# The first MLP product by one level of Strassen's rule, in 258-token tiles

## The chip, the cores and the metric

The kernel runs on one core of one Trainium2 chip. The metric is the device time of one execution in microseconds. The hardware profile is of one execution. TensorE is shown as two rows: PE for the matmuls, PEld for the loads of the stationary operand; DVE is VectorE, ACT is ScalarE, POOL is GpSimd, SP is SyncE, which issues most transfers.

## The reference

One decoder layer over 1024 prompt tokens and 8 decode tokens, 1032 in all, of width 1024, with shared weights. A wide projection feeds a pooling branch, a chunked mLSTM with four heads and an attention into 256 memory tokens; their outputs are gated, merged and projected. The change touches what comes last:

```python
x = x + rmsnorm(merged @ w_out, g_post_mix)
h2 = rmsnorm(x, g_pre_mlp)
f = jnp.square(jax.nn.relu(h2 @ w_ff1)) @ w_ff2      # w_ff1 (1024, 4096), w_ff2 (4096, 1024)
x = x + rmsnorm(f, g_post_mlp)
```

All is fp32. The kernel keeps that precision with a split: an operand is held as a rounded high part and a low part (the rest), and a product is three matmuls: high by high, low by high, high by low.

## The kernel before

Everything is feature-major: 128 features on the partitions, 1032 tokens along the row, in three groups of 344 (`tok[g]`). Weights come as slabs of 128 x 1024 values (`w_raw`, two slots), loaded by SP; GpSimd, at times ScalarE, makes the high part `w_hi` and GpSimd the low part `w_lo` (`split`, `split_merge`). All engines run lists written out by hand, one block per engine, with semaphores between them; loops (`Fori`) repeat three times in the MLP.

The work ends so. TensorE forms z = merged @ w_out in groups of 24 matmuls of 344 columns (8 blocks of the contraction, 3 passes). ScalarE copies and squares z, VectorE scales it by the inverse deviation (`z_scale`, recorded at line 1178, the helper of all scalar_tensor_tensor operations), GpSimd adds it to x (`x_in`, line 541): that is x1. ScalarE squares x1 into a ring, TensorE sums the squares over the features with a matrix of ones (line 838), ScalarE takes the root, VectorE the reciprocal (line 1525) and scales x1 into `acc`; ScalarE makes `h_hi`, VectorE and GpSimd four blocks of `h_lo` each (lines 1531 and 547). All of this goes group by group.

The MLP runs in eight chunks of 512 hidden features. `ff1` makes four column blocks for three groups: 24 matmuls each; ScalarE takes relu out of the bank, VectorE squares (1540), ScalarE rounds to `f_hi` and VectorE makes `f_lo` (1542), in two halves by turns. `ff2` takes the chunk of before in eight blocks by three groups of 12 matmuls, and VectorE adds each bank to `acc` (line 1552). On TensorE every matmul of a split product is recorded at line 581. In the tail the squares of the last blocks are summed by matmuls (`f_mean`, line 887), VectorE takes a reciprocal for each group (line 1570) and scales, and VectorE and GpSimd add x1 back.

GpSimd has two operations of 1024 elements for every slab. In SP's queue the slabs stand in order, each behind the split of the one before last.

## Time and profile before

| | |
|---|---|
| time, median of 3 runs | 2194.12 us (2193.63 to 2194.25) |
| profiled execution: span | 2186.1 us |
| what lies around the span, against the median | 8.0 us |
| TensorE matmuls busy | 2065.8 us (94%) |
| VectorE, GpSimd, ScalarE busy | 965.5, 801.9, 458.5 us |
| first matmul of the MLP | 1420.0 us |
| DMA | 180.16 MB, 82 GB/s over the span |

A matmul is recorded longer than the distance to the next one, since they are pipelined: the pace is read from starts, not from the mean length. A chain of waits is followed back from the end. Idle time of an engine that is not on that chain costs nothing.

### The profile page before, as it was taken

The page shows a single profiled execution, that of the slowest core. Times are in us where ns is not written, and L with a number is a line of the kernel's source. Part 1 is how long each engine was busy: PE and PEld are TensorE (multiplying, and loading weights), DVE is VectorE, ACT ScalarE, POOL GpSimd, SP SyncE. Part 2 cuts the span into 40 slices and gives each one's busy share as a digit, 9 for nine tenths or more (in the row PEclk, how much of TensorE's full clock was granted, in tenths as well). Part 3 has the DMA queues.
Part 4 walks back from the last instruction along what each step waited for, and adds up shares of the span by engine and source line. Part 5 has one row for each costly group of instructions (what it writes and reads, how often), then busy time and mean ns, then how long its engine had stood idle before and what let it go on. Part 6 is the DMA issues. An engine that isn't in the chain of part 4 may idle for free.

```text
span 2186.1 us, 32789 instructions
## 1 busy us (share of the span) xinstructions
PE 2065.8 (94%) x12821; PEld 2006.9 (92%) x12821; DVE 965.5 (44%) x1884; ACT 458.5 (21%) x880; POOL 801.9 (37%) x407
## 2 busy tenths in 40 slices
PE   5799999999999999999899989599999999999996
PEld 3799999999999999999889889399999999999995
DVE  6602552055403551155666741974334343443426
ACT  4411220122012220122046422431101010110101
POOL 4553323323333233332522233754334343343433
PEclk8899999999999999999889999799999999999998
DMA  3221331123211331123645331121111111111132
GB/s 136 68 81 60 111 125 64 39 102 115 97 39 64 125 125 40 49 102 125 223 133 162 97 128 47 58 78 43 45 49 50 48 39 50 49 49 44 44 116 78
DMA packets 64142, 180.16 MB, mean 82 GB/s; under 512 B 6648, under 2 KB 22264, under 8 KB 63400
## 3 DMA queue, kind: packets, MB, share of 16 engines
q1 hardware_dynamic: 57664, 154.46, 20.9%
q10 hardware_dynamic: 6376, 24.14, 2.8%
q8 instruction: 88, 1.44, 0.3%
q14 instruction: 14, 0.11, 0.0%
HBM read 141.83 MB, written 36.75 MB: 82 GB/s over the span
## 4 chain that ended last, share of the span: by engine, by line
PE 85%; DVE 9%; issue 2%; ACT 2%; DMA 1%; POOL 1%; SPq 0%; DVEq 0%; ACTq 0%; POOLq 0%
PE bank L581 77%; DVE acc L1178 2%; PE bank L705 1%; PE bank L708 1%; DVE x_in L1178 1%; PE bank L693 1%; PE bank L664 1%; PE bank L701 1%; PE bank L696 1%; DMA x_in<-xT 1%; PE bank L703 0%; PE bank L778 0%; PE bank L838 0%; PE bank L801 0%; PE bank L745 0%
## 5 line engine op out<-in xcount | busy, mean ns | idle before, releaser
L581 PE MATMUL bank<-h_hi,w_hi 128*128 128x344 f32 x2520 | 823.5, 327 | 29.1 <-DVE h_lo L1193 14.5
L581 PE MATMUL bank<-h_lo,w_hi 128*128 128x344 f32 x2520 | 807.6, 320 | 0.0
L581 PE MATMUL bank<-h_hi,w_lo 128*128 128x344 f32 x2520 | 805.8, 320 | 0.4 <-issue 0.4
L478 POOL TENSOR_TENSOR w_hi<-w_raw,ones 128x1024 fp32r<-128x1024 f32 x152 | 288.8, 1900 | 1193.1 <-PE bank L581 1180.4
L581 PEld LDWEIGHTS bank<-h_hi,w_hi 128*128 128x128 f32 x2520 | 475.8, 189 | 36.8 <-DVE h_lo L1193 15.0
L581 PEld LDWEIGHTS bank<-h_hi,w_lo 128*128 128x128 f32 x2520 | 475.4, 189 | 2.3 <-issue 1.0
L581 PEld LDWEIGHTS bank<-h_lo,w_hi 128*128 128x128 f32 x2520 | 475.7, 189 | 0.0
L480 POOL TENSOR_TENSOR w_lo<-w_raw,w_hi 128x1024 fp32r<-128x1024 f32 x152 | 371.6, 2445 | 11.9
L581 PE MATMUL bank<-f_hi,w_hi 128*128 128x344 f32 x768 | 246.4, 321 | 0.0
L581 PE MATMUL bank<-f_hi,w_lo 128*128 128x344 f32 x768 | 245.4, 320 | 0.0
L581 PE MATMUL bank<-f_lo,w_hi 128*128 128x344 f32 x768 | 245.2, 319 | 0.0
L1552 DVE TENSOR_TENSOR acc<-acc,bank 128x344 f32<-128x344 f32 x192 | 97.1, 511 | 230.0 <-PE bank L581 229.9
L1540 DVE TENSOR_TENSOR sqv<-rl 128x344 f32<-128x344 f32 x96 | 93.0, 969 | 142.2 <-ACT rl L904 141.8
L581 PEld LDWEIGHTS bank<-f_hi,w_hi 128*128 128x128 f32 x768 | 144.4, 188 | 0.8
L581 PEld LDWEIGHTS bank<-f_lo,w_hi 128*128 128x128 f32 x768 | 144.3, 188 | 0.0
L581 PEld LDWEIGHTS bank<-f_hi,w_lo 128*128 128x128 f32 x768 | 144.0, 188 | 0.2
L904 ACT ACTIVATE rl<-bank 128x344 f32<-128x344 f32 x96 | 43.8, 457 | 421.9 <-PE bank L581 421.9
L1542 DVE TENSOR_TENSOR f_lo<-sqv,f_hi 128x344 fp32r<-128x344 f32 x96 | 98.6, 1027 | 53.6 <-ACT f_hi L1139 53.6
L904 ACT ACTIVATE side_t<-bank 128x344 f32<-128x344 f32 x96 | 43.9, 458 | 309.1 <-PE bank L581 309.1
L1312 DVE TENSOR_TENSOR SW<-bank,SW 128x128 f32<-128x128 f32 x32 | 9.3, 292 | 143.1 <-ACT SW L1017 143.1
L1139 ACT ACTIVATE f_hi<-sqv 128x344 fp32r<-128x344 f32 x96 | 47.2, 492 | 117.7 <-DVE sqv L1540 117.7
L904 ACT ACTIVATE o_h<-bank 128x344 f32<-128x344 f32 x40 | 18.3, 459 | 234.3 <-PE bank L581 230.5
(293 smaller groups left out, 2442.2 us busy)
## 6 DMA issues: line engine op xcount, KB each, us to landing
w_raw<-w_stream SPq DMA_DIRECT2D x161, 512.0 KB, 3.3
d_side<-side_t ACTq DMA_DIRECT2D x32, 516.0 KB, 2.7
gates<-d_side SPq DMA_DIRECT2D x24, 344.0 KB, 4.2
dC<-stC SPq DMA_DIRECT2D x32, 256.0 KB, 3.4
qkb<-d_qk SPq DMA_DIRECT2D x32, 256.0 KB, 4.0
o_C_s<-dC SPq DMA_DIRECT2D x32, 256.0 KB, 2.0
x_in<-xT SPq DMA_DIRECT2D x3, 1376.0 KB, 11.2
gates<-d_side SPq DMA_DIRECT2D x8, 516.0 KB, 4.0
```

Source lines behind the costliest of these rows:

```text
L478: pool.tensor_tensor(w_hi[:, slot, :], w_raw[:, slot, :], ones[:, 0:1].to_broadcast([P, 1024]), ALU.mult).then_inc(s_hi_made, 1)
L480: pool.tensor_tensor(w_lo[:, slot, :], w_raw[:, slot, :], w_hi[:, slot, :].bitcast(F32), ALU.subtract)\
L581: last = pe.matmul(out, st, mv, start=i == 0, stop=i == n - 1)
L664: last = pe.transpose(b_tr[r][:, (c % 2) * 256 + k * P:(c % 2) * 256 + (k + 1) * P], src[:, k, c * L:(c + 1) * L], ident[:, :])
L693: last = pe.matmul(b_S[:, 0:L], ks[:, k, :], qs[:, k, :], start=k == 0, stop=k == 1)
L696: pe.matmul(b_W[:, 0:L], ones[0:4, :], A_pick[:, :], start=False, stop=True).then_inc(s_logw_ready, 1)
L904: act.activation(out, bank[g + 3 * second][:, 0:G], func, scale=scale).then_inc(s_group_free[g], 1)
L1139: act.activation(f_hi[:, half, j, tok[g]], sqv[:, g, :], ACT.Copy).then_inc(s_f_hi, 1)
L1178: return dve.scalar_tensor_tensor(out=out, in0=in0, scalar=scalar, in1=in1, op0=op0, op1=op1)
L1540: dve.tensor_tensor(sqv[:, g, :], rl[:, g, :], rl[:, g, :], ALU.mult).then_inc(s_relu_squared, 1)
L1542: dve.tensor_tensor(f_lo[:, half, j, tok[g]], sqv[:, g, :], f_hi[:, half, j, tok[g]].bitcast(F32), ALU.subtract).then_inc(s_f_lo, 1)
L1552: dve.tensor_tensor(acc[:, j, tok[g]], acc[:, j, tok[g]], bank[g + 3 * second][:, 0:G], ALU.add).then_inc(s_group_free[g], 1)
```

## The change

The first product is cut into halves in all three directions. Weights: two column blocks of w_ff1 form a pair, 16 in all, with two halves of the contraction; x1 has the same two contraction halves and two token halves of 516, each worked in two tiles of 258. One level of Strassen's rule gives each pair 7 products instead of 8. Each product needs a sum or difference of quarters of the weights (`W_OF`, 5 of 7; made on GpSimd per pair, in a ring of 8 slots of 512) and of x1 (`B_OF`, 5 of 7; made once on VectorE, in `build`, and kept). A product is 12 matmuls for each tile (4 contraction blocks, 3 passes), into a ring of 8 banks. ScalarE copies the first three products' tiles (`copy_c`), VectorE adds or subtracts the others (`combine`; steps d, e and f read a bank). At the end of a quarter, step u does relu and the scaling by the inverse deviation of x1; ScalarE squares it into a stage (`make_f`), and SP writes two rows of 1032 to DRAM for each pair (`store_f`).

So x1 is no longer scaled ahead of the product: ScalarE writes x1 times the gain into `acc`. The combining tiles `c_t` and the weights of odd pairs (`w_pairB`) also lie in acc's room, and the sums are made out of acc in the first pair. The second product runs after the first, in four chunks of 1024 hidden features: 32 units of three groups of 24 matmuls, whose rows are read back from DRAM and split again (ScalarE high, GpSimd low). The first chunk's rows land over the operands of the first product, as its last pair frees them. Loops in this part are written out. Semaphores are shared more widely elsewhere in the kernel, without a change of order there. `f_mean` is one matmul for each group, of squares that VectorE has summed, and the order of the last blocks changes.

The diff, cut to its core:

```diff
+        W_OF = [((0, 0), ALU.add, (1, 1)), ((1, 1), None, None), ((0, 0), ALU.add, (0, 1)), ((0, 1), ALU.subtract, (1, 1)),
+                ((0, 0), None, None), ((1, 0), ALU.add, (1, 1)), ((1, 0), ALU.subtract, (0, 0))]
+        B_OF = [((0, 0), ALU.add, (1, 1)), ((1, 0), ALU.subtract, (0, 0)), ((1, 1), None, None), ((1, 0), ALU.add, (1, 1)),
+                ((0, 1), ALU.subtract, (1, 1)), ((0, 0), None, None), ((0, 0), ALU.add, (0, 1))]
...
+        def w_quarter(i, q):
+            return (w_raw, w_pairB)[i % 2][:, q[0], 512 * q[1]:512 * q[1] + 512]
+
+        def b_quarter(q, s):
+            return acc[:, 4 * q[0]:4 * q[0] + 4, HALF * q[1] + Q4 * s:HALF * q[1] + Q4 * (s + 1)]
...
+        C_STEPS = [(1, 0, "d"), (1, 1, "d"), (2, 0, "d"), (2, 1, "d"), (3, 0, "d"), (3, 1, "d"), (3, 0, "u"), (3, 1, "u"),
+                   (4, 0, "f"), (4, 0, "e"), (4, 1, "f"), (4, 1, "e"), (4, 0, "u"), (4, 1, "u"),
+                   (5, 0, "f"), (5, 0, "e"), (5, 1, "f"), (5, 1, "e"), (5, 0, "u"), (5, 1, "u"),
+                   (6, 0, "e"), (6, 1, "e"), (6, 0, "u"), (6, 1, "u")]
...
+
+            i, p, s = t // 14, t % 14 // 2, t % 2
+            copied = 6 * i + 2 * p + s + 1 if p < 3 else 0
+            stepped = c_step(i, (p, s, "d" if p < 4 else "e")) if p else 0
+            return copied, stepped
...
+            def pair(i):
+                if i == 0:
+                    sp.wait_ge(s_slab_split, SLAB_FF)
+                elif i == 1:
+                    sp.wait_ge(s_b_lo, 10)
+                else:
+                    sp.wait_ge(s_wc_sum, 5 * (i - 1))
+                    sp.wait_ge(s_wc_lo, 7 * (i - 2) + 5)
+                sp.dma_start((w_raw, w_pairB)[i % 2][:, :, :],
+                             w_stream[SLAB_FF + 2 * i:SLAB_FF + 2 * i + 2].rearrange("a p c -> p a c"))\
+                    .then_inc(s_pair_loaded[i % 2], 16)
+
+            def store_f(i):
+                sp.wait_ge(s_f_made, 8 * (i + 1))
+                for m in range(2):
+                    sp.dma_start(d_f[2 * i + m], f_st[i % 2][m]).then_inc(s_f_stored[i % 2], 16)
...
+            for i in range(PAIRS - 1):
+                if i + 2 < PAIRS:
+                    pair(i + 2)
+                store_f(i)
+            for r in range(4):
+                sp.wait_ge(s_tile, 14 * (PAIRS - 1) + 2 * r + 2)
+                if r >= 2:
+                    sp.wait_ge(s_f_row_hi, 2 * r - 2)
+                sp.dma_start(f0_raw[:, 2 * r:2 * r + 2, :], d_f[2 * r:2 * r + 2].rearrange("a p t -> p a t"))\
+                    .then_inc(s_f_row[r % 2], 16)
+                if r >= 2:
+                    w2_slab(3 - r)
...
+                    sp.wait_ge(s_f_row_hi, 8 + u if j < 2 else 7 + u)
+                    sp.dma_start(f_raw[(c + 1) % 2][:, j, :], d_f[8 * (c + 1) + j]).then_inc(s_f_row[j % 2], 16)
...
+            def wc_sum(n):
+                i, p = n // 7, n % 7
...
+                pool.wait_ge(s_pair_loaded[i % 2], 16 * (i // 2 + 1))
+                if n == 5:
+                    pool.wait_ge(s_group_ready[2], UNIT_OUT + 8)
+                elif n >= RING:
+                    pool.wait_ge(s_tile, 2 * (n - RING) + 2)
+                pool.tensor_tensor(ring_sum[n % RING], w_quarter(i, a), w_quarter(i, b), op).then_inc(s_wc_sum, 1)
+
+            def wc_lo(n):
+                i, p = n // 7, n % 7
+                pool.wait_ge(s_wc_hi, n + 1)
+                t = w_quarter(i, W_OF[p][0]) if W_OF[p][1] is None else ring_sum[n % RING]
+                pool.tensor_tensor(ring_lo[n % RING], t, ring_hi[n % RING].bitcast(F32), ALU.subtract).then_inc(s_wc_lo, 1)
...
+            for n in range(4, 7 * PAIRS):
+                wc_sum(n + 1)
+                wc_lo(n)
...
+            for r in range(6):
+                f_row_lo(r, r + 1)
+                if r >= 4:
+                    w2_split(r - 4)
+            w2_split(2)
+            for u in range(32):
+                if u + 3 < 32:
+                    w2_split(u + 3)
+                if u < 24:
+                    f_row_lo(8 + u, 8 + u + 1)
...
-            def ff1(n, slots, t, first=0):
-                for j in range(first, 4):
-                    pe.wait_ge(s_slab_split, n + j + 1)
-                    for g in range(NG):
-                        h_group(slots[j], g, t + j)
...
+            for i in range(PAIRS):
+                for p in range(7):
+                    n = 7 * i + p
+                    pe.wait_ge(s_wc_lo, n + 1)
+                    for s in range(2):
+                        t = 2 * n + s
+                        if i == 0:
+                            pe.wait_ge(s_b_lo, 2 * p + s + 1)
+                        if t >= 8:
+                            copied, stepped = tile_read(t - 8)
+                            if copied:
+                                pe.wait_ge(s_c_copied, copied)
+                            if stepped:
+                                pe.wait_ge(s_c_step, stepped)
+                        product(bank[t % 8][:, 0:Q4],
+                                [(ring_hi[n % RING][:, k * P:(k + 1) * P], ring_lo[n % RING][:, k * P:(k + 1) * P],
+                                  b_hi[p][:, k, sub[s]], b_lo[p][:, k, sub[s]]) for k in range(4)]).then_inc(s_tile, 1)
+
+            def ff2_group(u, g, bank_of=None):
+                c, slot = u // 8, u % 4
+                group(g, UNIT_FF + u, [(w2_hi[slot][:, k * P:(k + 1) * P], w2_lo[slot][:, k * P:(k + 1) * P],
+                                        f_hi[c % 2][:, k, tok[g]], f_lo[c % 2][:, k, tok[g]]) for k in range(KD)], True, bank_of)
+            pe.wait_ge(s_c_step, c_step(PAIRS - 1, (4, 0, "e")))
+            pe.wait_ge(s_f_row_lo_dve, 2)
+            for u in range(28):
+                if u % 8 == 0:
+                    pe.wait_ge(s_f_row_lo, 6 + u)
+                pe.wait_ge(s_w2_lo, u + 1)
+                for g in range(NG):
+                    ff2_group(u, g)
...
+                if op is None:
+                    act.wait_ge(s_pair_loaded[i % 2], 16 * (i // 2 + 1))
+                    if n == 4:
+                        act.wait_ge(s_group_ready[2], UNIT_OUT + 8)
+                    elif n >= RING:
+                        act.wait_ge(s_tile, 2 * (n - RING) + 2)
+                    src = w_quarter(i, a)
+                else:
+                    act.wait_ge(s_wc_sum, wc_sums(n))
+                    src = ring_sum[n % RING]
+                act.activation(ring_hi[n % RING], src, ACT.Copy).then_inc(s_wc_hi, 1)
+
             for i, (j, g) in enumerate(z_last):
...
                     act.activation(sq_ring(i % 6), x_in[:, k, tok[g]], ACT.Square).then_inc(s_x1_sq, 1)
-                    if g == 1 and k == 3:
-                        x1_root(0)
+                    act.activation(acc[:, k, tok[g]], x_in[:, k, tok[g]], ACT.Copy, scale=vec[:, V_MLP + k:V_MLP + k + 1])\
+                       .then_inc(s_xg, 1)
+                    if g and k == 3:
...
+                    t = 14 * i + 2 * p + s
+                    if i:
+                        act.wait_ge(s_f_made, 8 * (i - 1) + 7 - 2 * p + s)
+                    act.wait_ge(s_tile, t + 1)
+                    act.activation((c1, c4, c5)[p][s], bank[t % 8][:, 0:Q4], ACT.Copy).then_inc(s_c_copied, 1)
...
+                if p == 3 and i >= 2:
+                    act.wait_ge(s_f_stored[i % 2], 32 * (i // 2))
+                for s in range(2):
+                    act.wait_ge(s_c_step, c_step(i, (p, s, "u")))
+                    act.activation(f_st[i % 2][m][:, HALF * half + Q4 * s:HALF * half + Q4 * (s + 1)], src[s], ACT.Square)\
+                       .then_inc(s_f_made, 1)
...
+            b_high(0)
+            for i in range(PAIRS):
+                for p in range(7):
+                    n = 7 * i + p
+                    if i == 0 and p == 0:
+                        b_high(1)
+                        wc_high(4)
+                        wc_high(5)
+                        for q in (2, 3, 4):
+                            b_high(q)
+                    elif i == 0 and p == 1:
+                        b_high(5)
+                    wc_high(n + 6)
+                    if i == 0 and p == 0:
+                        act.wait_ge(s_b_lo, 10)
+                    if p == 0 and i:
+                        make_f(i - 1, 6)
+                    if p < 3:
+                        copy_c(i, p)
+                        if i == 0 and p == 2:
+                            b_high(6)
+                    if p > 3:
+                        make_f(i, p - 1)
+                    if i == PAIRS - 1 and p >= 4:
+                        f_row_high(2 * p - 8)
+                        f_row_high(2 * p - 7)
+            make_f(PAIRS - 1, 6)
+            w2_high(0)
+            w2_high(1)
+            f_row_high(6)
+            f_row_high(7)
+            w2_high(2)
...
+                a, op, b = B_OF[p]
+                for s in range(2):
+                    if op is not None:
+                        if p == 6:
+                            dve.wait_ge(s_x1_stored, 16)
+                        dve.tensor_tensor(b_sum[p][:, :, sub[s]], b_quarter(a, s), b_quarter(b, s), op).then_inc(s_b_sum, 1)
+                for s in range(2):
+                    dve.wait_ge(s_b_hi, 2 * p + s + 1)
+                    t = b_quarter(a, s) if op is None else b_sum[p][:, :, sub[s]]
+                    dve.tensor_tensor(b_lo[p][:, :, sub[s]], t, b_hi[p][:, :, sub[s]].bitcast(F32), ALU.subtract).then_inc(s_b_lo, 1)
+
...
+                for step_ in [x for x in C_STEPS if x[0] == p]:
+                    _, s, what = step_
+                    t = 14 * i + 2 * p + s
+                    m = bank[t % 8][:, 0:Q4]
+                    if what == "u":
+                        if (i, p, s) == (0, 3, 0):
+                            for g in range(NG):
+                                dve.wait_ge(s_x1_std, g + 1)
+                                last = dve.reciprocal(rstd0[:, tok[g]], rstd0b[:, tok[g]])
+                            step(last)
+                        tile_, half, made = {3: (d_t, 0, "d"), 4: (c5, 1, "f"), 5: (c4, 0, "f"), 6: (c1, 1, "e")}[p]
+                        dve.wait_ge(s_c_step, c_step(i, (p, s, made)))
+                        stt(tile_[s], tile_[s], 0.0, rstd0[:, HALF * half + Q4 * s:HALF * half + Q4 * (s + 1)], ALU.max, ALU.mult)\
+                            .then_inc(s_c_step, 1)
...
+            combine(0, 1)
+            build(5)
+            combine(0, 2)
+            build(6)
+            for p in range(3, 7):
+                combine(0, p)
+            for i in range(1, PAIRS):
+                for p in range(1, 7):
+                    combine(i, p)
+
```

VectorE where the MLP begins. Before, after the scaling of z (scalings, reciprocals and low parts of x1, then the squares of the first blocks):

```order
L1178 SCALAR_TENSOR_TENSOR acc<-acc,vec,rstd 128x344 x8
L1525 RECIPROCAL rstd<-rstd0b 128x344
L1178 SCALAR_TENSOR_TENSOR acc<-x_in,vec,rstd 128x344 x8
L1531 TENSOR_TENSOR h_lo<-acc,h_hi 128x344 x4
L1525 RECIPROCAL rstd<-rstd0b 128x344
L1178 SCALAR_TENSOR_TENSOR acc<-x_in,vec,rstd 128x344 x8
L1531 TENSOR_TENSOR h_lo<-acc,h_hi 128x344 x4
L1525 RECIPROCAL rstd<-rstd0b 128x344
L1178 SCALAR_TENSOR_TENSOR acc<-x_in,vec,rstd 128x344 x8
```

In the changed kernel, at the same place (bA, bC and bD are x1's operands, c_t the combining tiles, 128x4x258 is 1032 elements):

```order
L1391 SCALAR_TENSOR_TENSOR acc<-acc,vec,rstd 128x344 x8
L1742 TENSOR_TENSOR bA_raw<-acc 128x4x258 x2
L1746 TENSOR_TENSOR bA_lo<-bA_raw,bA_hi 128x4x258 x2
L1742 TENSOR_TENSOR bA_raw<-acc 128x4x258 x2
L1746 TENSOR_TENSOR bA_lo<-bA_raw,bA_hi 128x4x258 x2
L1746 TENSOR_TENSOR bA_lo<-acc,bA_hi 128x4x258 x2
L1742 TENSOR_TENSOR bA_raw<-acc 128x4x258 x2
L1746 TENSOR_TENSOR bA_lo<-bA_raw,bA_hi 128x4x258 x2
L1742 TENSOR_TENSOR bC_raw<-acc 128x4x258 x2
L1746 TENSOR_TENSOR bC_lo<-bC_raw,bC_hi 128x4x258 x2
L1776 TENSOR_TENSOR c_t<-c_t,bank 128x258 x2
L1746 TENSOR_TENSOR bD_lo<-acc,bD_hi 128x4x258 x2
```

and right behind it:

```order
L1776 TENSOR_TENSOR c_t<-c_t,bank 128x258 x2
L1742 TENSOR_TENSOR bD_raw<-acc 128x4x258 x2
L1746 TENSOR_TENSOR bD_lo<-bD_raw,bD_hi 128x4x258 x2
L1776 TENSOR_TENSOR c_t<-c_t,bank 128x258 x2
L1760 RECIPROCAL rstd<-rstd0b 128x344 x3
L1391 SCALAR_TENSOR_TENSOR c_t<-c_t,rstd 128x258 x2
L1781 TENSOR_TENSOR c_t<-c_t,bank 128x258
L1785 TENSOR_TENSOR c_t<-c_t,bank 128x258
```

The reciprocals move from ahead of the first product to behind the steps of the fourth (p = 3), and 10 sums and 14 low parts stand ahead of them.

ScalarE between the first product and the second. Before, it alternates inside the chunk:

```order
L1142 ISA
L904 ACTIVATE rl<-bank 128x344
L1138 REGISTER_ALU
L1139 ACTIVATE f_hi<-sqv 128x344
L904 ACTIVATE rl<-bank 128x344
```

In the changed kernel (the last pair; sq, rstd0b and zsq hold the stages of squares, f_raw the rows that come back, w2's slots are wcD, w_x and w):

```order
L1303 ACTIVATE rstd0b<-c_t 128x258 x2
L1316 ACTIVATE f_hi<-f_raw 128x1032 x2
L1303 ACTIVATE rstd0b<-c_t 128x258 x2
L1316 ACTIVATE f_hi<-f_raw 128x1032 x2
L1303 ACTIVATE zsq<-c_t 128x258 x2
L1316 ACTIVATE f_hi<-f_raw 128x1032 x2
L1303 ACTIVATE zsq<-c_t 128x258 x2
L1308 ACTIVATE wcD_hi<-wcD_raw 128x1024
L1308 ACTIVATE w_x_hi<-w_raw 128x1024
L1316 ACTIVATE f_hi<-f_raw 128x1032 x2
```

The high parts of the rows stand between the squares of the last pair, each behind a square that waits for VectorE.

GpSimd, before, at the MLP's start and in the changed kernel between the two products:

```order
L547 TENSOR_TENSOR h_lo<-acc,h_hi 128x344 x12
L478 TENSOR_TENSOR w_hi<-w_raw,ones 128x1024
L480 TENSOR_TENSOR w_lo<-w_raw,w_hi 128x1024
L478 TENSOR_TENSOR w_hi<-w_raw,ones 128x1024
L480 TENSOR_TENSOR w_lo<-w_raw,w_hi 128x1024
L552 MEMSET acc 128x8256
```

```order
L675 TENSOR_TENSOR w_lo_raw<-w_pairB 128x512
L681 TENSOR_TENSOR w_lo<-w_lo_raw,w_hi 128x512 x2
L698 TENSOR_TENSOR f_lo<-f_raw,f_hi 128x1032 x5
L703 TENSOR_TENSOR wcD_lo<-wcD_raw,wcD_hi 128x1024
L698 TENSOR_TENSOR f_lo<-f_raw,f_hi 128x1032
L703 TENSOR_TENSOR w_x_lo<-w_raw,w_x_hi 128x1024
L703 TENSOR_TENSOR w_lo<-w_lo_raw,w_hi 128x1024 x2
```

Six low parts of rows and the first weight split are now one series there, where before the splits of slabs ran along with the products.

## Rows read from the trace of the kernel before

**Rows 1.** The page: busy time (share, instructions), and the chain that ended last
```profile
PE 2065.8 (94%) x12821; PEld 2006.9 (92%) x12821; DVE 965.5 (44%) x1884; ACT 458.5 (21%) x880; POOL 801.9 (37%) x407
...
PE 85%; DVE 9%; issue 2%; ACT 2%; DMA 1%; POOL 1%; SPq 0%; DVEq 0%; ACTq 0%; POOLq 0%
```

**Rows 2.** Stretches of the span, inside and ahead of the MLP (columns in the header)
```profile
core 0: us, PE busy (x) PEld busy (x) DVE busy (x) ACT busy (x) POOL busy (x), PEclk, DMA share, GB/s
...
1370.00:1412.00 42.00, 17.90 (x60) 11.76 (x58) 41.86 (x40) 15.89 (x34) 35.95 (x30) 0.71 0.08 25
...
1460.00:1640.00 180.00, 180.00 (x1145) 179.84 (x1145) 75.50 (x98) 25.35 (x54) 66.37 (x31) 1.00 0.15 48
```

**Rows 3.** Timeline of TensorE at the memory's product (start, length, idle before)
```profile
68.37 0.28 PE L581 MATMUL bank<-m_hi,w_hi 128*128 128x256 f32 x1
...
70.98 0.28 PE L581 MATMUL bank<-m_lo,w_hi 128*128 128x256 f32 x1
73.24 0.38 PE L581 MATMUL bank<-m_hi,w_hi 128*128 128x256 f32 x1 [1.98 <-POOL w_lo L474]
...
73.89 0.42 PE L581 MATMUL bank<-m_hi,w_lo 128*128 128x256 f32 x1
...
76.67 0.41 PE L581 MATMUL bank<-m_lo,w_hi 128*128 128x256 f32 x1
...
77.10 0.29 PE L581 MATMUL bank<-m_hi,w_lo 128*128 128x256 f32 x1
...
80.40 0.28 PE L581 MATMUL bank<-m_lo,w_hi 128*128 128x256 f32 x1
```

**Rows 4.** Timelines of GpSimd and TensorE around the MLP's start
```profile
1391.24 2.36 POOL L474 TENSOR_TENSOR w_lo<-w_raw,w_hi 128x1024 fp32r<-128x1024 f32 x1
1394.05 8.89 POOL L541 TENSOR_TENSOR x_in<-x_in,acc 128x344 f32<-128x344 f32 x8 [0.45 <-DVE acc L1178]
...
1419.99 0.58 PE L581 MATMUL bank<-h_hi,w_hi 128*128 128x344 f32 x1
```

**Rows 5.** Single lines: count, ns least/median/most, first and last start, form
```profile
L541 POOL TENSOR_TENSOR x_in<-x_in,acc x24: 907/1179/1199, 1371.2 to 1402.0; 128x344 f32<-128x344 f32 x24
L480 POOL TENSOR_TENSOR w_lo<-w_raw,w_hi x152: 2343/2403/2562, 13.4 to 2130.8; 128x1024 fp32r<-128x1024 f32 x152
L1178 DVE SCALAR_TENSOR_TENSOR acc<-x_in,vec,rstd x24: 562/1218/2060, 1403.6 to 1432.3; 128x344 f32<-128x344 f32 x24
L1552 DVE TENSOR_TENSOR acc<-acc,bank x192: 498/512/515, 1517.4 to 2164.1; 128x344 f32<-128x344 f32 x192
L1401 DVE TENSOR_TENSOR win_a<-u_pad x2: 1222/1678/2133, 1079.7 to 1088.4; 128x1032 f32<-128x1032 f32 x2
L1125 ACT ACTIVATE sq<-x_in x24: 472/477/492, 1381.8 to 1415.4; 128x344 f32<-128x344 f32 x24
```

**Rows 6.** Table of lines: form, count, busy us, mean ns, idle before
```profile
L1338 DVE TENSOR_TENSOR num<-num,bank 128x257 f32<-128x257 f32 x32 | 13.4, 418 | 0.0
...
L1073 ACT ACTIVATE gates<-gates 128x1032 f32<-128x1032 f32 x8 | 8.4, 1056 | 0.7 <-DMA gates<-d_side 0.7
...
L954 ACT ACTIVATE mem_in<-bank 128x256 f32<-128x256 f32 x8 | 3.0, 381 | 16.1 <-PE bank L581 16.0
```

**Rows 7.** DMA issues: KB each, median us to landing
```profile
d_x<-x_in ACTq DMA_DIRECT2D x1, 4128.0 KB, 11.3
...
o_kv<-mem_in ACTq DMA_DIRECT2D x1, 1024.0 KB, 5.4
```

**Rows 8.** Timelines of TensorE and VectorE in the tail
```profile
2143.64 1.90 PE L887 MATMUL bank<-rl,ones 128*128 128x344 f32 x6
...
2148.01 0.58 PE L581 MATMUL bank<-f_hi,w_hi 128*128 128x344 f32 x1
...
2160.42 0.74 PE L887 MATMUL bank<-sqv,ones 128*128 128x344 f32 x2
...
2171.62 2.29 DVE L1570 RECIPROCAL rstd<-rstd0b 128x344 f32<-128x344 f32 x1
```

613 lines of the change are left out of this document (330 added, 283 removed).

## The prediction

> **What bounds the kernel now.** I read the page first. TensorE is busy for 94% of the span and the chain that ended last is 85% TensorE, 77% of it line 581, the helper in which all split products are recorded [rows 1]. So the question is how fast TensorE gets its products, and where it stands still. Each of the two products of the MLP has 2304 matmuls (32 column blocks, 3 token groups, 8 contraction blocks, 3 passes). A stretch inside the MLP shows 180 us with 1145 matmuls and the full clock, 2.4 GHz: one per 157.2 ns [rows 2]. The MLP's 4608 matmuls are then 724 us; they run from 1420.0 [rows 4] to 2160.4, where the last square sum begins [rows 8], and the rest of these 740.4 us is two square sums of 4.4 us each and pauses of one or two microseconds. Ahead of 1420.0 lies the other place of interest: from 1370 to 1412 TensorE is busy for 17.9 of 42 us, at a mean clock of 0.71, while VectorE is busy for 41.9 [rows 2].
>
> **The arithmetic that goes.** The new first product needs 16 pairs of 7 products of 2 tiles of 12 matmuls, 2688 of them, of 258 columns. That is 17% more instructions and 12.5% fewer columns, so everything hangs on whether a matmul with fewer columns is shorter, since each still brings its own weight load, and the weight loads are busy almost as long as the matmuls [rows 1]. The trace has a neighbour: the memory's product with 256 columns. Its first burst takes 2.61 us for 23 steps, 113.5 ns; the end of the next 3.30 us for 28, 118 ns; both at 2.4 GHz, and 213.8 ns at 1.2 GHz (2.78 us for 13) after an idle stretch [rows 3]. So the length does follow the columns. For 258 columns the ends are 114.3 ns (113.5 plus two columns of 0.42 ns) and 121.4 ns (157.2 less 86 such columns). I take 118.0, three quarters of 157.2, which is also the second burst. A pair is 168 matmuls, 19.8 us; fifteen are 297.4 us (288.0 to 305.9).
>
> The Trainium skill ("TensorE: Matmul & The Clock Gate", Back-to-back issue gap) gives columns divided by 2.4 GHz plus 2.5 ns for one matmul after another. At 256 columns that is 109.2 ns where the rows show 113.5 to 118; at 344 it is 145.8 where they show 157.2, so the trace runs longer than the rule both times. By it the fifteen pairs would take 277 us, 20 us less than my sum.
>
> **The start.** Before, VectorE takes a reciprocal for each group (2.29 us, as in [rows 8]), scales eight blocks and makes half of the low parts, one group after another; the first product starts at 1420.0 [rows 4]. Now ScalarE writes x1 times the gain into acc as soon as x1 is there, and the inverse deviation is applied after the product. x1's last additions took 8.89 us for eight on GpSimd, since they alternate with VectorE's scalings, and ended at 1402.9; the weight split of 2.36 us ahead of them held VectorE's first scaling up [rows 4]. That split and its like go. Seven small operations on weight halves stand ahead of group 0; those that come late cost 1 us there, which the wait for group 1's scalings absorbs. I put the last x1 at 1401.6 and its scaled copy at 1402.6 (two ScalarE operations, 0.48 us each, [rows 5]). First sum, high part and low part of a 1032-wide half operand: 1.22 us on VectorE [rows 5], 1.05 on ScalarE [rows 6], 1.2 again, with ScalarE's last root between: the first tile starts at 1407.5, 12.5 us earlier than before.
>
> **The first pair.** Here TensorE isn't the limit. VectorE must make 10 sums and 14 low parts of 1032 elements. At 1.2 us they are 28.8 us, against 19.8 us of TensorE, and its order puts five operands ahead of the first combining step. GpSimd works meanwhile on weight halves of 512: 0.907 us for 344 and 2.343 for 1024 [rows 5] make 2.11 ns per element and 1.26 us for 512, 1.2 in a row. With each other's two-input operations they take turns: the scaling lasts 562 ns alone and 1218 with GpSimd in between [rows 5]. Step by step: 18 operations, 21.6 us, and four of GpSimd, 4.8 us, from 1402.6: 1429. Only then does pair 1 load, into room inside acc; 1 MB took 5.4 us [rows 7], and behind it come GpSimd's sum, ScalarE's high part (0.6, between its rows for 256 and 1032) and two copies (0.38 each, [rows 6]), which the first combining step waits for in ScalarE's order: 1437. Then 0.8 us of steps, the sixth operand (two operations and two of GpSimd, 4.9), 0.8, the seventh (four, 4.8): 1448.5, and its last tile ends at 1450. Now the three reciprocals stand in VectorE's queue, between product 3's steps and its scalings: 0.8 + 6.9 + 3.4 for two scalings with GpSimd ahead of each + 0.8 = 1460.5. Behind them is the release of the bank that TensorE needs for the second product of pair 1; TensorE has done the first of it by 1452.8, so the pause is about 7.5 us. With 2.5 us more of small pauses while VectorE catches up, pair 1 as a whole starts as if at 1460: the first pair costs 52.5 us instead of 19.8. Its ends: 38 us (all GpSimd turns and ScalarE's waits hidden, only 28.8 + 6.9 + 2) and 66 us (VectorE's operations and GpSimd's strictly in turn, 24 times 2.4, and 8 behind it). x1's store, which the last operands wait for, took 11.3 us [rows 7] and is done by 1415: it costs nothing.
>
> **The pairs after it.** Per pair of 19.8 us: GpSimd has 12 operations, 14.4 us. ScalarE has 7 high parts (0.6), 6 copies (0.38) and 8 squares (0.4), 9.7 us. VectorE has 16 steps that read a bank, at 418 ns for 257 columns [rows 6], 6.7 us; GpSimd doesn't hold these up, since the additions that read a bank have 498, 512 and 515 ns as least, median and most [rows 5] although GpSimd splits beside them. It also has 8 scalings with two SBUF inputs, 0.48 us and a wait for GpSimd of nothing to a whole operation, for which I take half (0.63): 8.9 us, so 15.6 together. Both are covered by the products, and eight banks and eight weight slots give six products of lead. SP loads 1 MB and stores 1 MB per pair, at 5.4 us for 1 MB covered. From both sides VectorE has 9.0 us (no wait) to 22.8 us per pair (16 of 512 ns, 8 of 1.83).
>
> **The hand-over to the second product.** The eight rows of the first chunk overwrite operands, so they come back product by product. ScalarE makes rows 0 to 5 high between the squares of the last pair, with rows 4 and 5 not before the end of the first product (E): its third load waits for the high part of row 1. GpSimd then has six low parts of 1032 (2.4 us each) and one 1024 split ahead of the first unit, from about E - 5: 16.8 us, with VectorE's last scalings and low parts between them 2 more: E + 14. TensorE stands 14 us and then runs at 1.2 GHz for a few us, 2 us more: 16 (9 to 21). The ends are ScalarE's own chain (last square, two splits, two rows: 9 us) and a late load ahead of all of it.
>
> **Second product and tail.** 2304 matmuls at 157.2 ns, 362.2 us, as before. In a unit of 11.3 us GpSimd has one split and one low part, 4.8 us, ScalarE at most 3.5 us; the last row of a chunk is loaded and split within one unit (4.5 us landing, 2 ScalarE, 4.8 GpSimd: 11.3 at worst), so 0 to 6 us over three boundaries; I take 0. Square sums on VectorE need one matmul per group instead of eight: 1.2 us in place of two times 4.4 [rows 8] ahead of the end. The tail is VectorE's chain of three reciprocals and 24 scalings, 11.2 us from the last group to the last reciprocal and 14.5 from there [rows 8]; it stays, 0.5 us longer.
>
> **The sum.** 1407.5 + 52.5 + 297.4 + 16 + 362.2 + 1.2 = 2136.8, against 2160.4 for the last group before: 23.6 earlier, 23.1 after the tail. The profiled execution's span is 2186.1 and the median of the runs 2194.12, 8.0 more for what lies around it; 2194.12 - 23.1 is 2171.0. I forecast 2171 us.
>
> **Rivals.**
> The lock decides in every pair (slower). If VectorE's scalings always find GpSimd in the port, and a step costs 512 ns, VectorE is the bound at 22.8 us a pair: 15 x 3.0 = 45 us more, 2215. It is slower than before from 21.3 us a pair (19.8 + 23.1/15). For it: the turns that the two engines take [rows 4, 5], and 14.4 us of GpSimd per pair. Against it: GpSimd is ahead of its ring and then idle, and only 8 of 24 steps are concerned.
> The Trainium skill ("SBUF — State Buffer", SBUF: two separate sides) calls this port an exclusive lock, held for the whole instruction by whichever of the two engines starts first. The trace agrees, with 562 against 1218 ns, and it speaks for this rival.
> Loads and splits at the seams cost more: a first pair of 60 us, a hand-over of 20, and 4 us at the chunk boundaries: 2186.
> Everything at the seams overlaps and the spacing is 114.3 ns: 10 less in the first pair, 4 in the hand-over, 9 in the spacing: 2147.
> The columns save nothing, and 258 costs the weight load's pace as 344 does (157.2): 2520 x 39 ns = 99 us more, 2269. The 256-column bursts speak against it.
> The skill's back-to-back rule would give 2150; the rows at 256 and 344 columns both refuse it.
>
> **Chances.** Forecast as summed 0.55, with its own range of 2157 to 2182; lock 0.14; dear seams 0.13; cheap seams 0.13; the skill's spacing 0.03; no column saving 0.02. What a measurement of this kernel can tell from no change is 0.2%, 4.4 us. Faster is the forecast, both cheap cases and most of the dear seams, 0.81; the same 0.05; slower is the lock's larger part and the last case, 0.14. The range takes in the dear seams and the cheap ones in part: 2148 to 2196.
>
> **What would show it.** In the changed profile: 258-column matmuls 118 ns apart at full clock; the first near 1407; pair 1 starting near 1457 behind a pause that ends with VectorE's release after three reciprocals; fifteen pairs at 19.8 us with no idle; about 14 us idle ahead of the second product, ended by GpSimd's low parts; scalings of c_t that last 0.5 to 1.7 us, bank steps always 0.42. The forecast falls if a pair takes over 21 us, or if the first pair and the hand-over together cost over 90.

## The result, and the profile of the changed kernel

| | time, median (lowest to highest) | span of the profiled execution |
|---|---|---|
| before, 5 runs | 2193.63 us (2188.38 to 2194.25) | 2186.1 us |
| changed, 5 runs | 2181.79 us (2178.22 to 2184.58) | 2177.0 us |

The ratio is 0.995, with a 95% interval of 0.9937 to 0.9963. The kernel became faster by 0.5%, about half of what was forecast (2171): the time lies in the range, on the side forecast, 10.8 us above the number. I read the trace from its end back to the place where the first product starts, and compare stretches, not ends: what lies ahead of the MLP differs between executions by several microseconds, as shown further down.

The page of the changed kernel, answering to [rows 1]: busy time, and the chain that ended last.

```profile
PE 2031.5 (93%) x13163; PEld 1972.3 (91%) x13163; DVE 963.5 (44%) x1970; ACT 599.0 (28%) x1124; POOL 914.5 (42%) x522
...
PE 82%; DVE 10%; issue 2%; ACT 2%; DMA 2%; POOL 1%; SPq 0%; DVEq 0%; ACTq 0%; POOLq 0%
```

TensorE is 34 us less busy, but its share of the chain fell from 85 to 82%: part of what it no longer computes it waits for. Stretches of the changed kernel, answering to [rows 2] (start:end, length, busy us and instructions of each engine, granted clock, DMA share, GB/s):

```profile
1370.00:1412.00 42.00, 29.06 (x90) 16.38 (x89) 39.17 (x35) 29.00 (x62) 32.67 (x29) 0.83 0.18 76
1412.00:1457.00 45.00, 28.13 (x181) 26.83 (x180) 37.05 (x32) 18.08 (x28) 21.02 (x12) 0.80 0.18 71
1480.00:1640.00 160.00, 160.00 (x1338) 160.00 (x1337) 113.16 (x197) 72.23 (x171) 129.43 (x99) 1.00 0.30 107
...
1758.00:1776.00 18.00, 1.19 (x10) 1.01 (x9) 14.41 (x13) 10.76 (x15) 14.48 (x7) 0.64 0.73 263
1776.00:1781.00 5.00, 5.00 (x20) 5.00 (x21) 0.00 (x0) 2.01 (x2) 5.00 (x3) 0.58 0.05 19
```

Inside the first product TensorE isn't idle at all, at the full clock, one matmul per 119.8 ns (from the starts). Ahead of it, behind it and in the first pair it is. The list of TensorE's waits from 1400 on names them (what waited, for whom, us in total, times, longest):

```profile
PE bank L732 <- DVE f_lo L1802: 16.8, 1, 16.8
PE bank L1025 <- DVE frb L1823: 10.9, 2, 8.3
PE bank L732 <- DVE bA_lo L1746: 6.7, 3, 3.5
PE bank L732 <- DVE bD_lo L1746: 6.1, 1, 6.1
PE bank L732 <- DVE acc L1807: 4.7, 2, 4.0
PE bank L732 <- DVE c_t L1785: 3.9, 1, 3.9
```

The first is the hand-over, the third, fourth and sixth are the first pair; all these were in the sum. Of the second, 8.3 us are the tail, which was in the sum, and 2.6 us a pause ahead of a square sum, which wasn't. Nor was the fifth. TensorE's timeline has these waits with their time (start, us, what, idle before and who ended it); the first row answers to [rows 4], the last two to [rows 8]:

```profile
1409.23 0.55 PE L732 MATMUL bank<-bA_hi,wcA_hi 128*128 128x258 f32 x1 [3.46 <-DVE bA_lo L1746]
...
1775.84 0.63 PE L732 MATMUL bank<-f_hi,wcD_hi 128*128 128x344 f32 x1 [16.81 <-DVE f_lo L1802]
...
2064.88 0.62 PE L732 MATMUL bank<-f_hi,w_x_hi 128*128 128x344 f32 x1 [4.00 <-DVE acc L1807]
...
2143.62 0.85 PE L1025 MATMUL bank<-frb,ones 128*128 128x344 f32 x2 [2.60 <-DVE frb L1823]
...
2160.35 0.94 PE L1025 MATMUL bank<-frb,ones 128*128 128x344 f32 x1 [8.35 <-DVE frb L1823]
```

Who held VectorE's line 1807 stands in its own timeline, and in the DMA issues of that stretch (KB, us to landing), which answer to [rows 7]:

```profile
2049.61 0.51 DVE L1807 TENSOR_TENSOR acc<-acc,bank 128x344 f32<-128x344 f32 x1 [3.26 <-PE bank L732]
2064.22 0.93 DVE L1807 TENSOR_TENSOR acc<-acc,bank 128x344 f32<-128x344 f32 x2 [14.10 <-DMA x_back<-d_x]
```

```profile
x_back<-d_x SPq DMA_DIRECT2D x1, 4128.0 KB, 14.2
```

The additions of line 1807 need nothing of this load. VectorE's wait for x1 stands in its program ahead of the loop over the last 24 groups, since the additions to x1 come in that loop; the bank releases of these groups are behind it. In the kernel before, the load was issued later still (2111.3), but the wait stood behind all but four of the last additions. Now its room holds rows of the second product until unit 24, so it is issued at 2050.0, inside the loop's first groups. TensorE used up its free banks, stood for 4.0 us, and then had 18 matmuls at the low clock (287 ns in place of 157).

The statistics of VectorE's combining lines, answering to [rows 5] (times ns least/median/most, first and last start):

```profile
L1391 DVE SCALAR_TENSOR_TENSOR c_t<-c_t,rstd x128: 414/1012/2635, 1455.7 to 1764.9; 128x258 f32<-128x258 f32 x128
L1776 DVE TENSOR_TENSOR c_t<-c_t,bank x96: 411/424/426, 1436.9 to 1750.4; 128x258 f32<-128x258 f32 x96
L1785 DVE TENSOR_TENSOR c_t<-c_t,bank x96: 407/410/419, 1456.8 to 1762.8; 128x258 f32<-128x258 f32 x96
```

The scalings (two SBUF inputs) do wait for GpSimd, the steps that read a bank don't, and inside the pairs they leave TensorE alone.

At the hand-over, VectorE's timeline has the last two scalings and its two low parts:

```profile
1763.08 4.43 DVE L1391 SCALAR_TENSOR_TENSOR c_t<-c_t,rstd 128x258 f32<-128x258 f32 x2
1770.84 4.90 DVE L1802 TENSOR_TENSOR f_lo<-f_raw,f_hi 128x1032 fp32r<-128x1032 f32 x2 [3.33 <-ACT f_hi L1316]
```

Between them ScalarE squares the last tile, makes two weight slabs high and then rows 6 and 7. The low parts end at 1775.74, 0.1 us before TensorE starts.

### The profile page after: what moved, and what is told of

It reads as the page before. It is cut to its first block, busy times and chain, and to the rows that moved or that the text cites. A ratio compares the mean times of both kernels' runs of the same rounds, so it can differ in the third digit from the quotient of the medians.

```text
span 2177.0 us, 33857 instructions
## 1 busy us (share of the span) xinstructions
PE 2031.5 (93%) x13163; PEld 1972.3 (91%) x13163; DVE 963.5 (44%) x1970; ACT 599.0 (28%) x1124; POOL 914.5 (42%) x522
## 4 chain that ended last, share of the span: by engine, by line
PE 82%; DVE 10%; issue 2%; ACT 2%; DMA 2%; POOL 1%; SPq 0%; DVEq 0%; ACTq 0%; POOLq 0%
PE bank L732 73%; DVE acc L1391 2%; PE bank L856 1%; PE bank L859 1%; DVE x_in L1391 1%; PE bank L844 1%; DMA x_back<-d_x 1%; PE bank L815 1%; PE bank L852 1%; PE bank L896 1%; PE bank L847 1%; DMA x_in<-xT 1%; PE bank L854 0%; DVE h_lo L1686 0%; DVE c_t L1391 0%
## 5 line engine op out<-in xcount | busy, mean ns | idle before, releaser
L732 PE MATMUL bank<-h_hi,w_hi 128*128 128x344 f32 x1752 | 576.2, 329 | 19.8 <-DVE h_lo L1406 14.4
L732 PE MATMUL bank<-h_lo,w_hi 128*128 128x344 f32 x1752 | 561.3, 320 | 0.0
L732 PE MATMUL bank<-h_hi,w_lo 128*128 128x344 f32 x1752 | 559.6, 319 | 0.0
L732 PEld LDWEIGHTS bank<-h_hi,w_hi 128*128 128x128 f32 x1752 | 330.5, 189 | 26.9 <-DVE h_lo L1406 15.0
L732 PEld LDWEIGHTS bank<-h_hi,w_lo 128*128 128x128 f32 x1752 | 330.3, 189 | 1.2
L732 PEld LDWEIGHTS bank<-h_lo,w_hi 128*128 128x128 f32 x1752 | 330.5, 189 | 0.0
L608 POOL TENSOR_TENSOR w_lo<-w_raw,w_hi 128x1024 fp32r<-128x1024 f32 x90 | 217.8, 2420 | 7.0
L1391 DVE SCALAR_TENSOR_TENSOR c_t<-c_t,rstd 128x258 f32<-128x258 f32 x128 | 134.1, 1086 | 0.0
L732 PE MATMUL bank<-f_hi,w_hi 128*128 128x344 f32 x384 | 123.2, 321 | 0.7 <-DVE acc L1807 0.7
L732 PE MATMUL bank<-f_hi,w_lo 128*128 128x344 f32 x384 | 122.4, 319 | 0.0
L732 PE MATMUL bank<-f_hi,wcD_hi 128*128 128x344 f32 x192 | 62.4, 325 | 16.8 <-DVE f_lo L1802 16.8
```

Source lines behind the costliest of these rows:

```text
L608: pool.tensor_tensor(w_lo[:, slot, :], w_raw[:, slot, :], w_hi[:, slot, :].bitcast(F32), ALU.subtract)\
L732: last = pe.matmul(out, st, mv, start=i == 0, stop=i == n - 1)
L1391: return dve.scalar_tensor_tensor(out=out, in0=in0, scalar=scalar, in1=in1, op0=op0, op1=op1)
```

## The experiments

Each kernel is the changed one with one edit unless it says otherwise. "Z" is VectorE's first reciprocal of the mixer's output, the last point ahead of the change that all kernels share. All numbers but the medians come from one profiled execution of each, in us: from Z to the first tile; first product (from its first to its last matmul); the stand behind it; second product (first to last matmul); from there to the end of the span; and the sum of the last four.

| kernel | Z to tile | first | stand | second | tail | tile to end | median, ratio to before (95%) |
|---|---|---|---|---|---|---|---|
| before | 51.8 | | | | 25.8 | 766.1 | |
| before again | 51.3 | | | | | 765.8 | |
| changed | 40.8 | 349.5 | 17.1 | 375.8 | 25.3 | 767.8 | 2181.79, 0.995 (0.9937 to 0.9963) |
| e1 wait moved | 40.8 | 349.2 | 17.1 | 369.1 | 25.3 | 760.7 | 2174.65, 0.9929 (0.9907 to 0.995) |
| e2 tail order | 40.8 | 349.1 | 17.1 | 366.4 | 24.8 | 757.3 | 2173.11, 0.9908 (0.9887 to 0.9928) |
| e3 hand-over | 40.8 | 349.2 | 7.1 | 377.5 | 25.3 | 759.1 | 2168.62, 0.9896 (0.9878 to 0.9914) |
| e4 scalings later | 40.8 | 347.1 | 16.8 | 373.9 | 25.3 | 763.2 | 2180.31, 0.9954 (0.9938 to 0.9969) |
| e6 last group | 40.8 | 349.2 | 17.1 | 366.3 | 24.5 | 757.1 | 2173.84, 0.9918 (0.99 to 0.9936) |
| e7 all | 40.8 | 346.8 | 10.2 | 365.9 | 24.5 | 747.4 | 2162.18, 0.9852 (0.9828 to 0.9876) |
| e8 reciprocals early | 40.8 | 345.5 | 17.1 | 376.6 | 25.3 | 764.4 | 2177.77, 0.9937 (0.9921 to 0.9953) |
| e9 scaled first | 55.9 | 344.6 | 17.1 | 375.9 | 25.3 | 762.9 | 2192.67, 1.0008 (0.9995 to 1.0022) |
| e10 all, early | 40.8 | 342.3 | 7.1 | 367.4 | 24.5 | 741.2 | 2152.41, 0.9827 (0.9803 to 0.9852) |

Where nothing was edited, the first product and the tail repeat within 0.4 us from kernel to kernel. The second product does so less: behind each stand TensorE runs some matmuls at 1.2 GHz, 287 instead of 157 ns apart, and their number differs between executions (12 to 17 such distances behind the unedited stand of 17.1 us), 0.13 us for each. The medians are of 4 to 12 runs. Their intervals overlap between the changed kernel, e4 and e8, between e1, e2 and e6, and by a little between the changed kernel and e1: effects as small as those of e2, e4, e6 and e8 rest on one profile each.

**e1, the wait moved.**

```diff
-            dve.wait_ge(s_x3_loaded, 16)
             for i in range(24):
 ...
                     if q == 0:
+                        dve.wait_ge(s_x3_loaded, 16)
                         y_add(0)
```

> From the changed kernel, one line moved: VectorE waits for the reload of x1 (4.1 MB, lands 14.2 us after it is issued) only ahead of the first addition to it, no longer ahead of the 24 bank additions of the last eight units. My theory: this wait is the largest part of what the second product takes above 362 us. VectorE stood 14.1 us, TensorE ran out of banks, stood 4.3 us at 2064.9 and then had 18 matmuls at the low clock (2.3 us). With the wait moved the pause and the slow matmuls go, and the span is 6.5 us shorter than the changed kernel's 2177.0: 2170.5. Rival A: the reload itself is what holds TensorE, since it shares the queues with the weight slabs of units 25 to 28; then a pause of some us stays at 2065 to 2075, ended by a weight split, and the gain is under 2 us. Rival B: the time is given back in the tail, where VectorE is behind anyway: the last group ends 6.5 us earlier but the span is shorter by under 2 us.

Measured: 7.1 us less from the first tile to the end, 6.7 of it in the second product. VectorE's timeline over the stretch in which it had stood for 14.1 us:

```profile
2047.95 0.51 DVE L1807 TENSOR_TENSOR acc<-acc,bank 128x344 f32<-128x344 f32 x1 [3.26 <-PE bank L732]
2051.73 0.51 DVE L1807 TENSOR_TENSOR acc<-acc,bank 128x344 f32<-128x344 f32 x1 [3.26 <-PE bank L732]
2055.50 0.51 DVE L1807 TENSOR_TENSOR acc<-acc,bank 128x344 f32<-128x344 f32 x1 [3.25 <-PE bank L732]
```

It follows its groups at 3.77 us. The list of TensorE's waits from 1770 to 2140 in the same kernel:

```profile
PE bank L732 <- DVE f_lo L1802: 16.8, 1, 16.8
PE bank L1025 <- DVE frb L1823: 2.6, 1, 2.6
PE bank L732 <- DVE acc L1807: 0.7, 1, 0.7
```

No pause ended by a weight split takes its place (rival A falls), and the tail keeps its length (rival B falls). The wait is the cause.

**e2, the order of the tail** (with the edit of e1).

```diff
-                if i in (18, 22):
-                    y_inverse(q); y_scale(q, range(4))
-                elif i in (19, 23):
-                    y_scale(q, range(4, KD)); y_add(0) for q == 0
+                if i in (18, 22):
+                    y_inverse((i - 18) // 4)
+                elif i in (19, 20, 21, 23):
+                    y_scale(q, ((0, 1, 2), (3, 4, 5), (6, 7))[i - 19 - 4 * q])
+                    if i == 21:
+                        y_add(0)
             add_square(23)
+            y_scale(1, range(3, KD))
             y_add(1)
```

> The edit of the moved wait, and in the last six groups VectorE spreads the scalings of token groups 0 and 1 over more of its bank additions (reciprocal behind group 18, three scalings behind 19, three behind 20, two and the additions to x1 behind 21; of token group 1 three behind the last, five behind the last square sum). My theory: the late additions at 2142.6 and 2155.4 come from seven or four scalings in a row in VectorE's order; they cost TensorE 2.9 us ahead of the square sum of token group 1 (and 0.8 at the low clock), and hold the last square sum from about 2153.5 to 2160.35. Without them the span is 3.5 us shorter in the middle and 3 to 4 at the end: 6.5 for the wait and 6 to 7 for the order, 2164. Rival: VectorE's work between the last group and the end is a fixed sum (16 scalings, two reciprocals), so what is taken from before the last square sum is put back behind it: no more than 3.5 below the kernel with the wait alone, 2167 to 2170.

Measured: 3.4 us below e1 in the profile. The pause of 2.6 us ahead of the second square sum is gone (2.7 less in the second product); the last square sum comes 4 us sooner behind the last group (4.7 in place of 8.7), but the end only 0.5: the five scalings put back stand ahead of the last reciprocal. The rival is right about the tail, the theory about the pause.

**e3, the hand-over.** The first weight slab comes behind rows 0 and 1 on every engine, and TensorE goes through unit 0 by blocks instead of by groups:

```diff
+            for blocks in ((0, 1, 2, 3), (4, 5), (6, 7)):
+                pe.wait_ge(s_f_row_lo, blocks[-1] + 1)     # rows 6, 7: s_f_row_lo_dve
+                for g in range(NG):
+                    for k in blocks: ...                   # 3 passes into bank[g]
-            for u in range(28):
+            for u in range(1, 28):
```

> From the changed kernel, the hand-over alone: the first weight slab of the second product is loaded and split earlier (behind rows 0 and 1 of the first chunk, and not behind row 4), its second slab's split goes behind row 5, and TensorE goes through the first unit in three sweeps over the three banks: blocks 0 to 3 as soon as rows 0 to 3 have their low parts, then 4 and 5, then 6 and 7. My theory: the 16.8 us stand at 1775.8 is a chain of splits on GpSimd and VectorE in turn, rows in series, so a start at the fourth row comes at 1765 to 1768, and rows 4 to 7 are made beside 5.7 and 2.8 us of products: 8 to 10 us less, span 2167 to 2169. Rival A: the chain is set by ScalarE's last squares and the loads behind them, 1767.9 for rows 6 and 7; TensorE starts early and then waits for the last rows as long as before; under 3 us less. Rival B: units 1 and 2 then wait for their splits, which stand behind rows 4 and 5 on GpSimd; 2 to 5 us less.

Measured: the stand is 10.0 us shorter, and the second product 1.7 longer, 8.7 in all: as the theory has it. TensorE doesn't wait for the later rows. Of the 1.7 us, 1.2 are a pause behind the first unit, when ScalarE, busy with high parts until then, has yet to copy the first bank; the rest is four more matmuls at the low clock:

```profile
1784.27 0.40 PE L733 MATMUL bank<-f_hi,w_x_hi 128*128 128x344 f32 x1 [1.07 <-ACT acc L1057]
```

GpSimd's timeline shows the chain that sets the start, one low part behind another at 2.5 us:

```profile
1757.10 5.00 POOL L698 TENSOR_TENSOR f_lo<-f_raw,f_hi 128x1032 fp32r<-128x1032 f32 x2 [11.19 <-ACT f_hi L1331]
1762.06 2.57 POOL L703 TENSOR_TENSOR wcD_lo<-wcD_raw,wcD_hi 128x1024 fp32r<-128x1024 f32 x1
1764.58 10.15 POOL L698 TENSOR_TENSOR f_lo<-f_raw,f_hi 128x1032 fp32r<-128x1032 f32 x4
```

**e4, scalings behind the bank steps** (`C_STEPS`: the two `u` steps of product 3, and with them the reciprocals, behind the steps of product 4).

> From the changed kernel, VectorE's order alone: the three reciprocals and the two scalings of product 3 stand behind the steps that read the banks of product 4, in every pair. My theory: the pause of 4.2 us at 1457.3 ends with a bank step that is queued behind 6.9 us of reciprocals and 2 scalings; with the step ahead of them the pause goes and the span is 3 to 4 us shorter, 2173.5. Rival: VectorE is behind by its whole work in the first pair, not by the order of it, so the pause only moves to the banks of product 5 or 6 of the first pair's successor: within 1.5 us of the changed kernel. In neither case do the later pairs change (20.1 us).

Measured: 2.4 us less in the first product. The pause at pair 1 is 1.9 us (from start to start), against 4.2 in the changed kernel and 2.7 in e1 to e3. The first product gives what lies between theory and rival. Another 1.9 us in the second product aren't shown to come from this edit: 1.4 of them are 11 fewer matmuls at the low clock behind the two stands (20 distances of 287 ns in place of 31), 0.3 a shorter pause at x1's wait. The median moved by 1.5 only.

**e5, the spacing by width.** The second product's units 8 to 11 with 258 columns, 12 to 15 with 172, 16 to 19 with 128.

> From the changed kernel, with some columns left out in the second product: units 8 to 11 multiply 258 of 344 columns, units 12 to 15 172, units 16 to 19 128 (the rest of each bank keeps older values). It measures by itself what I had to take from the memory's product: the spacing of matmuls with a weight load each, by width. If spacing is columns and a constant, the two widths already seen (157.15 ns at 344, 119.8 at 258) make 0.434 ns a column and 7.8 ns: 82.5 ns at 172 and 63.4 ns at 128. Rival, a floor: the weight load of 128 rows takes its own time whatever the columns, and the spacing stops falling at 172 or 128; the lines on weight loads would then be as long as the spacing. For 258 columns both expect 119.8.

Measured, from the distances of starts (288 of each narrower width): medians of 157 ns at 344, 120 at 258, 112 at 172, 213 at 128 columns. Three stretches, one inside each of the new widths:

```profile
1880.00:1905.00 25.00, 25.00 (x210) 25.00 (x209) 4.36 (x9) 5.82 (x6) 14.34 (x6) 1.00 0.34 112
1915.00:1940.00 25.00, 25.00 (x226) 25.00 (x226) 4.64 (x10) 7.32 (x8) 14.91 (x7) 1.00 0.37 128
1950.00:2000.00 50.00, 50.00 (x236) 50.00 (x236) 4.62 (x9) 6.37 (x6) 16.43 (x7) 0.50 0.19 64
```

The reader is to see 226 matmuls of 172 columns in the time of 210 of 258: the spacing stops falling. The rival is right that there is a floor, and 258 columns lie just above it. Its other sign isn't there: the records of the weight loads are 192 ns long at 172 columns, not 112, so no run shows that the weight load makes the floor. The Trainium skill ("TensorE: Matmul & The Clock Gate", LDWEIGHTS) has a weight load take its 128 columns divided by 1.2 GHz, 106.7 ns; the 112 ns here agree with that as the floor, within 5 ns. At 128 columns the clock was 1.2 GHz, so this width has no number at the full clock. At the low one its 213 ns are what 256 columns took too (213.8 [rows 3]): there half the columns save nothing.

**before again**, the kernel before, unchanged.

> The kernel before, unchanged, profiled a second time. In its first profile TensorE's clock rises to 2.4 GHz some 20 us before the merge begins, in all five profiles of kernels with the change it stays at 1.2 GHz there; from the last head's products to the merge it is 68.7 us against 75.3 to 75.4, although the change alters no operation there. If this follows from the change (semaphores and rooms that were rearranged), this profile shows 68.7 again; if it is chance, it may show 75. And how far the start of the first product lies from the same point tells how much of the runs' spread comes from ahead of the change: 1420 before, 1409 to 1415 in the others.

Measured: span 2192.3, 6.2 longer than the first profile; 75.3 us from the last head's products to the merge, as in the kernels with the change. Its first MLP matmul starts at 1426.5 instead of 1420.0, and 765.8 us lie behind it (766.1). Stretch 1100 to 1120 in the first profile of before, in this one, and in e8:

```profile
1100.00:1120.00 20.00, 18.34 (x86) 13.83 (x86) 11.73 (x35) 5.45 (x11) 0.26 (x1) 0.72 0.28 79
```

```profile
1100.00:1120.00 20.00, 17.90 (x64) 15.09 (x65) 10.47 (x28) 3.29 (x6) 1.98 (x2) 0.50 0.09 35
```

```profile
1100.00:1120.00 20.00, 18.35 (x87) 13.87 (x87) 11.15 (x34) 5.46 (x11) 0.00 (x0) 0.73 0.24 76
```

The same work, 86 matmuls or 64 in it, by whether the clock has risen. Both happen in both kernels: it is chance, and part of the spread between executions. It isn't all of it: the changed kernel's profile has the slow stretch as well (0.50) and reaches Z at 1368.5, against 1375.2 in this one.

**e6, the last group's additions on VectorE** (with e2's edits).

> The kernel with the moved wait and the tail in the new order, and the additions to x1 of the last token group all on VectorE, behind its scalings (none on GpSimd). My theory: the last eight scalings take 1.22 us each while GpSimd adds beside them and 0.49 us alone; 8 alone and 8 additions of 0.43 are 7.4 us instead of the 8.5 measured with GpSimd's help: 1.1 us less to the end. Rival: the store of the first five blocks, which GpSimd's additions released early, now starts later and is what ends last: no gain, or 1 us more.

VectorE's timeline at the end of e2, then of e6:

```profile
2160.18 7.26 DVE L1391 SCALAR_TENSOR_TENSOR acc<-acc,vec,frs 128x344 f32<-128x344 f32 x8
2167.36 1.36 DVE L1837 TENSOR_TENSOR x_back<-x_back,acc 128x344 f32<-128x344 f32 x3
```

```profile
2159.63 3.99 DVE L1394 SCALAR_TENSOR_TENSOR acc<-acc,vec,frs 128x344 f32<-128x344 f32 x8
2163.54 3.50 DVE L1840 TENSOR_TENSOR x_back<-x_back,acc 128x344 f32<-128x344 f32 x8
```

The 1.1 us are there (8.54 against 7.41 from first to last), and the stores take back 0.9: they are issued 1.28 us apart instead of 2.15, and the end lies 4.5 us behind the last addition instead of 3.7. 0.2 remain: the rival, nearly.

**e7, all of them** (e2, e3, e4, e6).

> All edits at once: the hand-over in three sweeps, the moved wait, the tail in the new order with the last additions on VectorE, and the reciprocals and the scalings of product 3 behind the bank steps of product 4. If the parts add, as my theory has it (8.7, 6.9, 3.3, 1.1 and 2.5 us in the profiles, each from the first tile or the hand-over to the end), the stretch from the first 258-column matmul to the end is 767.8 - 22.5 = 745.3 us and the median about 2160. Rival: with a shorter stand at the hand-over the chunk's next loads and splits are closer to their use, and pauses of 2 to 6 us appear in the first units or at a chunk's end: 748 to 752 us.

Measured: 747.4, two above the theory. The stand is 10.2 us instead of 7.1, since e4's later scalings hold the first rows' high parts up on ScalarE: they start 3.6 us ahead of the last tile's last matmul, against 6.8 in e3. e10, without e4's edit, has 7.1 again.

**e8, the reciprocals in the idle stretch.**

```diff
             for p in range(5):
                 build(p)
+            for g in range(NG):
+                last = dve.reciprocal(rstd0[:, tok[g]], rstd0b[:, tok[g]])
+            step(last)
             combine(0, 1)
```

> From the changed kernel, one thing moved in VectorE's order: the three reciprocals stand behind the operands of the first five products, ahead of the first combining step. There VectorE is idle for 7.15 us (it waits from 1429.8 to 1436.9 for ScalarE's copy behind the load of pair 1); the reciprocals took 6.8 us at 1449.1 to 1455.7, ahead of the bank step that ended TensorE's pause of 4.2 us at 1457.3. My theory: they fit into the idle stretch, the pause goes, and the first pair is shorter by 4 to 5 us (the tile of product 6, at 1447.4 in the changed kernel, isn't earlier); from the first tile to the end 763 us instead of 767.8. Rival: VectorE has other work piled up behind them (20 steps of 0.42 and scalings), which alone keeps TensorE waiting for banks in pair 1: 1 to 2 us gained.

The changed kernel's VectorE, as the edit found it:

```profile
1427.40 2.38 DVE L1746 TENSOR_TENSOR bC_lo<-bC_raw,bC_hi 128x1032 fp32r<-128x1032 f32 x2
1436.93 0.76 DVE L1776 TENSOR_TENSOR c_t<-c_t,bank 128x258 f32<-128x258 f32 x2 [7.16 <-ACT c_t L1295]
...
1449.09 6.62 DVE L1760 RECIPROCAL rstd<-rstd0b 128x344 f32<-128x344 f32 x3
```

Measured: 4.0 us less in the first product, no pause at pair 1. The theory holds for the pause; from the first tile to the end it is 764.4 instead of its 763. The second product is 0.8 longer (376.6), which isn't shown to be the edit's: six more matmuls ran at the low clock behind the two stands (37 distances of 287 ns in place of 31).

**e9, scaled ahead of the product.** The deviation as before; the later scaling stays, so the output is scaled twice.

```diff
+            for g in range(NG):
+                step(dve.reciprocal(rstd0[:, tok[g]], rstd0b[:, tok[g]]))
+                for k in range(KD):
+                    last = dve.tensor_tensor(acc[:, k, tok[g]], acc[:, k, tok[g]], rstd0[:, tok[g]], ALU.mult)
```

> From the changed kernel, one part undone: the inverse deviation is applied to x1 ahead of the first product, as in the kernel before (three reciprocals and 24 multiplications of 344 columns on VectorE, token group by token group), instead of behind it; the later scaling of the combined tiles stays, so the output is scaled twice and only the time is read. My theory: from the first z reciprocal to the first tile it was 51.8 us before and 40.8 now, and from the first tile to the end 766.1 before and 767.8 now: the whole gain of the change lies in that start, and Strassen's rule with its seams, as placed here, gives nothing. With the scaling ahead, the first tile starts 10 to 14 us later (the last group's root, a reciprocal of 2.3, eight multiplications of 0.43), of which the first pair gives back 4 us (no reciprocals in it): 6 to 10 us slower than the changed kernel, 2188 to 2192, which is no faster than before. Rival: the first pair is bound by VectorE's operands and would start as late but then run without pauses (more slack for weights and pair 1's load): less than 4 us slower.

Measured: the first tile 15.1 us later, 4.9 given back in the first product, 10.2 in all; the median is 2192.67, ratio 1.0008 (0.9995 to 1.0022): no faster than before. The delay is above the theory's 10 to 14 us and the sum just above its 6 to 10. TensorE's first tile in this kernel and, behind it, in e10:

```profile
1425.94 0.55 PE L732 MATMUL bank<-bA_hi,wcA_hi 128*128 128x258 f32 x1 [18.52 <-DVE bA_lo L1746]
```

```profile
1410.36 0.55 PE L736 MATMUL bank<-bA_hi,wcA_hi 128*128 128x258 f32 x1 [3.47 <-DVE bA_lo L1765]
```

What the theory claims holds: without the start, the change gives nothing. From the first tile to the end e9 is 3.2 us shorter than before (762.9 against 766.1) and its first tile lies 4.1 us later behind Z (55.9 against 51.8): the two nearly cancel. Not run was the other half of this test, the kernel before with its scaling behind the first product and no sums: how much of the 11.0 us it would gain is open.

**e10, all but e4, with the reciprocals and the operand of product 5 early.**

> All edits that helped in the profiles, without the late scalings of product 3 (in the kernel with all edits they held back the rows of the first chunk: the stand before the second product was 10.2 us there and 7.1 without them), with the reciprocals and the operand of product 5 ahead of the first combining step. My theory: against the kernel with all edits (747.4 us from the first tile to the end) 3 us less at the hand-over and 2 to 3 in the first pair: 741 to 743, median 2155 to 2157. Rival: with the operand and the reciprocals 9.4 us stand in an idle stretch of 7.15, so the release of banks for product 5 comes 2 us later and eats the gain: 745 to 747.

Measured: 741.2, as the theory has it; median 2152.41, ratio to before 0.9827 (0.9803 to 0.9852), against 0.995 of the changed kernel: 27 us between the two by the ratios, 26.6 in the profiles. From the first tile to the end it is 24.9 us shorter than before (741.2 against 766.1): with these seams the products gain too, and not the start alone. TensorE's longest waits in it:

```profile
PE bank L736 <- DVE c_t L1790: 7.5, 1, 7.5
PE bank L1031 <- POOL f_lo L701: 6.8, 1, 6.8
PE bank L736 <- DVE bA_lo L1765: 6.8, 3, 3.5
PE bank L1043 <- DVE frb L1841: 4.4, 1, 4.4
```

The rival's effect is there too: the wait in the first pair is now for the first combining step, 7.5 us, in place of 6.1 for an operand, 3.9 for the bank and 2.3 of issue behind it.

## Why the prediction was wrong

Against the profiled span of 2186.1 I forecast 2163.0; it is 2177.0. By the terms of the sum (what is left of the 14.0 is rounding):

| term | predicted | measured | difference |
|---|---|---|---|
| first tile | 1407.5 | 1409.2 | +1.7 |
| first pair | 52.5 | 47.7 | -4.8 |
| fifteen pairs, 2520 matmuls | 297.4 | 301.9 | +4.5 |
| stand at the hand-over | 14 | 17.0 | +3.0 |
| low clock behind it | 2 | 1.8 | -0.2 |
| second product | 362.2 | 374.1 | +11.9 |
| last group to the end | 27.4 | 25.1 | -2.3 |

**The step that failed is the second product, "362.2 us, as before", with 0 for pauses: it took 374.1.** I had looked at its splits and at the rows at the chunk boundaries, and these were right: no pause for the rows of the second, third or fourth chunk. I had not followed what the rooms do to the last load, nor asked what is queued behind VectorE's wait for it. 6.7 us are that wait (e1), 2.7 the late square sums and additions (e2), which had been squares on TensorE before and needed nothing of VectorE's scalings. The remaining 2.5 are a pause of 1.0 at 2109.8 and the smaller ones around the square sums. Neither of the prediction's own signs of failure would have caught it: a pair took 20.1 us (limit 21), and the first pair and the hand-over 66.5 (limit 90).

The other terms. The first tile, the pairs without idle, the stand ended by low parts, and the pause behind three reciprocals were as described, though that pause was 4.2 us instead of 7.5. VectorE's last low part (1775.7), not GpSimd's (1774.7), ended the stand. The first pair was 4.8 us too dear in the sum, the spacing 1.8 ns too small: 119.8 lies near the upper end that I had given (121.4), not at three quarters of 157.2. The two errors cancel, which is luck. The tail was 2.3 us cheaper. One bound in the working is wrong by its own terms: 16 steps of 0.418 us and 8 scalings of 0.48 make 10.5 us of VectorE per pair without any wait, not 9.0; the sum doesn't use it.

The 8.0 us "around the span" were not that. In every kernel with a profiled time 1.8 to 2.2 us lie around the span (1.9 in the changed one). One run of before took 2188.38; if it is the profiled one, as its distance of 2.3 us from the span suggests, the other 5.7 are the distance of this execution from the median. The spans differ by 9.1, the medians of five by 11.8; from Z on, where chance is out, it is 9.3 (11.0 less 1.7).

The rivals. **The lock** is there (scalings of 414 to 2635 ns), and in the pairs it is covered: VectorE is busy for 113.2 of 160 us. It does bite at the hand-over, for which I had put 2 us: five of the last six scalings of the first product meet low parts of 2.4 us and take 1.8 to 2.6 us each, and the last square waits for them. **Dear seams** was nearest in its number, 2186, though not by its seams: only the hand-over was near what it had (18.8 of 20), and the extra was not in the first pair or at the chunk boundaries. **Cheap seams**, **the skill's spacing** (by the rule of the Trainium skill, "TensorE: Matmul & The Clock Gate", Back-to-back issue gap, 110 ns for 258 columns, which the section itself has for a single gap and not for a stream of weight loads and matmuls; 119.8 measured) and **no column saving** are refuted by the spacing.

Where the gain went, in one sum from the first tile to the end of the last group: 40.2 us of TensorE saved by the rule (2304 at 157.2 less 2688 at 119.8), 8.8 by the square sums, 7.2 of small pauses before; spent again were 27.5 in the first pair (349.5 less 322.0), 17.1 at the hand-over and 13.6 in the second product. That leaves 742.4 against 740.4. What the kernel gained is the 11.0 us between Z and the first tile; e9, with the scaling back ahead of the product, has none of it.

## What to carry to other kernels

A wait placed ahead of a loop holds every instruction of the loop: when a change moves the load behind it, follow that load to its room and to all that is queued behind the wait. An arithmetic saving is worth what its seams leave: price filling and draining (here 45 us for 40 saved) with the same care as the steady state, and look for idle stretches of the busy engine ahead of its pile, as the 7.2 us that took the reciprocals. Compare profiles from a point that both kernels share, since one execution each can differ by 6 us ahead of any change.

## What the hardware showed beyond that

- With a weight load per matmul the spacing follows the columns from 344 to 258 (157 and 120 ns) and stops at 112 ns by 172: by this, tiles between 172 and some 240 columns (112 ns on the line through the two wider ones, an estimate) cost TensorE as much as 240. Below 172 the full clock has no number.
- In e5 the clock fell to 1.2 GHz behind a pause of 1.8 us and, with 128 columns per matmul, stayed there for the 61 us of these units although TensorE had no idle time in them (50.00 of 50.00 us busy at 0.50); with 344 columns again it was back at 2.4 GHz from 2010 on.
- The 20 us from 1100 ran at a mean clock of 0.72 or of 0.50 in the same program, by chance, and the stretch from the last head's products to the merge took 6.6 us more with the second (75.3 against 68.7).
